# Two-layer hybrid decoder trunk: differential attention's parts share breaks in the dense matmuls, nine times a tile in place of twelve

## The reference

```
s = jnp.einsum('bhmid,bhmjd->bhmij', q_blk, k)          # m = 0, 1
s = jnp.where(dist >= 0, s - m_h * dist, -jnp.inf)
p = jax.nn.softmax(s, axis=-1)
w = p[:, :, 0] - lam_full * p[:, :, 1]
o = jnp.einsum('bhij,bhjd->bhid', w, v)
```

## Time and profile before

| | |
|---|---|
| median of 3 runs | 1976.94 us (1976.61 to 1977.6) |
| the profiled execution | 1978.86 us |
| its span, first to last instruction | 1977.0 us |
| PE busy | 1932.0 us, 98% |
| POOL busy | 920.0 us, 47% |
| DVE busy | 655.9 us, 33% |
| ACT busy | 500.0 us, 25% |
| mean granted TensorE clock | 0.995 of full speed |

### The profile page before, as it was taken

One profiled execution on the slowest core, in us unless ns is written; L12 is line 12 of the kernel. 1 busy time (PEld: TensorE's weight loads), 2 busy tenths in 40 slices (PEclk: granted clock), 3 DMA queues, 4 the chain that ended last, 5 costly groups with the idle time before them and its releaser, 6 DMA issues.

```text
span 1977.0 us, 26185 instructions
## 1 busy us (share of the span) xinstructions
PE 1932.0 (98%) x10952; PEld 1561.1 (79%) x10952; DVE 655.9 (33%) x1234; ACT 500.0 (25%) x1006; POOL 920.0 (47%) x876
## 2 busy tenths in 40 slices
PE   6999999989999999999999999999899999999999
PEld 5887777767888888777888877778688888887787
DVE  1554223122111343553335561232221113435432
ACT  3110122122222343332321011221122224433220
POOL 4555433434555444344554544434345555444454
PEclk9999999999999999999999999999999999999999
DMA  7566444535655555655675655444455555564556
GB/s 274 153 190 191 130 140 136 144 112 150 170 169 168 166 155 150 212 153 161 213 227 150 193 168 150 138 132 137 129 148 170 165 169 167 150 224 138 154 172 196
DMA packets 92181, 326.95 MB, mean 165 GB/s; under 512 B 10174, under 2 KB 10912, under 8 KB 91040
## 3 DMA queue, kind: packets, MB, share of 16 engines
q0 software_dynamic: 41472, 151.01, 27.2%
q1 hardware_dynamic: 44288, 155.75, 26.1%
q10 hardware_dynamic: 6304, 18.52, 2.4%
HBM read 316.86 MB, written 8.39 MB: 165 GB/s over the span
## 4 chain that ended last, share of the span: by engine, by line
PE 90%; DVE 5%; ACT 4%; DMA 1%; issue 0%; SPq 0%; ACTq 0%; DVEq 0%
PE acc L488 75%; PE mix L761 1%; PE mix L558 1%; DVE slots L1355 1%; PE mix L574 1%; PE mix L780 1%; PE mix L853 1%; PE mix L564 1%; PE mix L808 1%; PE mix L739 1%; DMA slots<-in_x 1%; DVE slots L1351 1%; PE mix L709 1%; PE mix L591 1%; PE mix L540 1%; ACT L1047 1%
## 5 line engine op out<-in xcount | busy, mean ns | idle before, releaser
L449 POOL TENSOR_TENSOR w_lo<-w_raw,w_hi 128x512 fp32r<-128x512 f32 x576 | 754.5, 1310 | 723.7 <-DMA w_hi<-in_wstream 509.4
L488 PE MATMUL acc<-w_hi,actT_hi 128*128 128x512 f32 x1920 | 784.5, 409 | 13.5 <-ACT slots L932 13.0
L488 PE MATMUL acc<-w_hi,actT_lo 128*128 128x512 f32 x1920 | 752.2, 392 | 0.0
L488 PE MATMUL acc<-w_lo,actT_hi 128*128 128x512 f32 x1920 | 751.2, 391 | 0.0
L488 PEld LDWEIGHTS acc<-w_hi,actT_hi 128*128 128x128 f32 x1920 | 362.1, 189 | 104.5 <-issue 33.0
L488 PEld LDWEIGHTS acc<-w_hi,actT_lo 128*128 128x128 f32 x1920 | 361.7, 188 | 78.8
L488 PEld LDWEIGHTS acc<-w_lo,actT_hi 128*128 128x128 f32 x1920 | 362.8, 189 | 65.4
L431 POOL DMA_DIRECT2D w_hi<-in_wstream x288 | 163.8, 569 | 322.5 <-PE acc L488 318.1
L488 PE MATMUL acc<-actT_hi,w_hi 128*128 128x512 f32 x384 | 152.8, 398 | 0.0
L488 PE MATMUL acc<-actT_hi,w_lo 128*128 128x512 f32 x384 | 150.3, 391 | 0.0
L488 PE MATMUL acc<-actT_lo,w_hi 128*128 128x512 f32 x384 | 150.3, 391 | 0.0
(11 more groups left out here) (249 smaller groups left out, 1646.5 us busy)
## 6 DMA issues: line engine op xcount, KB each, us to landing
w_hi<-in_wstream POOLq DMA_DIRECT2D x288, 512.0 KB, 3.9
w_raw<-in_wstream SPq DMA_DIRECT2D x288, 512.0 KB, 4.5
out_x<-slots ACTq DMA_DIRECT2D x7, 1024.0 KB, 7.6
slots<-in_x SPq DMA_DIRECT2D x4, 1024.0 KB, 15.5
slots<-in_x ACTq DMA_DIRECT2D x1, 4096.0 KB, 17.8
slots<-out_x ACTq DMA_DIRECT2D x1, 4096.0 KB, 15.4
out_x<-slots ACTq DMA_DIRECT2D x4, 256.0 KB, 2.2
cf_sb<-in_cf ACTq DMA_DIRECT2D x1, 933.0 KB, 11.0
```

What stands on the lines that cost most here:

```text
L449: pool.tensor_tensor(w_lo[:, n % RING], w_raw[:, g % RAW, k], w_hi[:, g % HI, k].bitcast(F32), ALU.subtract).then_inc(w_ready, 1)
L488: last = nc.tensor.matmul(acc[b][:, :], lhsT, rhs, start=(k == 0 and i == 0), stop=(k == kts - 1 and i == 2))
```

## The change

In each tile of differential attention the scores of head h + 2 (h = 0, 1) are issued in the break of the turn of head h, behind it, and no longer in a break of their own behind the values of head h. The turn of head 3 is issued in the break of the values of head 2, behind them. The generator has 10 stages in place of 13 (one of them, the third, issues nothing, before and after), and `project` spreads these 10 over the same k-steps. `DIF_PE`, the order of TensorE's parts, follows. The orders of ACT and DVE, all waits, and all instructions stay as they are.

```diff
-DIF_PE = ["s0", "s1", "t0", "v0", "s2", "t1", "v1", "s3", "t2", "v2", "t3", "v3"]
+DIF_PE = ["s0", "s1", "t0", "s2", "v0", "t1", "s3", "v1", "t2", "v2", "t3", "v3"]
...
                 scores(1)
                 yield
                 yield
-                for h in H:
+                for h in range(2):
                     turn(h)
+                    scores(h + 2)
                     yield
                     values(h)
                     yield
-                    if h + 2 < HEADS:
-                        scores(h + 2)
-                        yield
+                turn(2)
+                yield
+                values(2)
+                turn(3)
+                yield
+                values(3)
+                yield
...
                     project(l, 14 + n, IN_KTS + 12 * n, 12, 0, ahead=y_ready, mixer=dif(l, TILES - 1 - n),
-                            stages=13, skip=(4 if n == 0 else 0), spread=(1.0, 0.8, 0.7, 0.6)[n])
+                            stages=10, skip=(4 if n == 0 else 0), spread=(1.0, 0.8, 0.7, 0.6)[n])
```

## The result

Eight timed runs of the changed kernel gave a median of 1982.56 us (1982.15 to 1984.06), eight of the kernel before 1976.93 us (1976.23 to 1978.15): +5.6 us, a ratio of 1.0030 with a 95% interval of 1.0019 to 1.0041. Forecast were 1981.1 us and a range of 1978.5 to 1983.2.

What follows compares the result with a forecast made beforehand. TensorE, busy 98% of the span, was taken to bound the kernel. Waits adding 4.7 us less 0.6 gained by joins gave +4.1 on 1976.94, so 1981.1 us, range 1978.5 to 1983.2.

Steps and rivals of the forecast that it cites:

- 1.35 and 1.02 us: TensorE's wait for w3 before the turn of head 3, in tiles 3 and 1 of each layer; 4.7 us added.
- 0.6 us saved: Joined breaks on TensorE: 0.02 us for each of 16 turn-and-scores joins, 0.03 for each of 8 values-and-turn joins.
- The 0.09 us at the entry of the scores: Extra delay before the scores' first matmul on TensorE, claimed to stay about the same behind a turn (0.10).
- rival 3: Joining breaks saves more, the scores' entry hidden behind the turns, 2 to 2.5 us: 1979.3; chance 0.12.
- the 0.28 us to spare in tile 2: In tile 2 the turn of head 3 is reached 3.75 us behind t2, against 3.47 needed: no wait.
- POOL's phase against t2: In tiles 3 and 1, set by the k-step ending at t2, the same in both versions, so seen durations were taken.
- nothing takes it up later, since TensorE waits for no clocked event in what follows: Claim about TensorE after the new waits: the time they add is not recovered later, so the sum stays +4.1 us.
- Rival 2: The clock falls after a stall in tile 3, 6.8 us at half clock losing 3.4 us in one layer: 1984.5; chance 0.04.
- 1980.2 to 1982.0: The interval around the forecast of 1981.1 us for the whole kernel, given chance 0.66.
- rival 1: More waits: a POOL collision at L1635 in tile 2, 1 or 3, +1.5 to 2 us: 1982.8; chance 0.12.

Runs made afterwards that it cites:

- Experiment 1: From the changed kernel, only the scores of heads 2 and 3 join the turns; values of head 2 and turn of head 3 keep own breaks: 1978.2 us, ratio 1.0003.
- experiment 3: The changed kernel with all its joins, plus an empty stage between the turn of head 2 and the joined break (11 stages): 1977.55 us, ratio 1.0000.
- experiment 4: The changed kernel with ACT taking the exponentials of head 3 ahead of its copy of head 2's turns: 1978.83 us, ratio 1.0006.
- Experiment 2: From the kernel before, only the turn of head 3 joins the values of head 2; scores keep own breaks (12 stages): 1990.94 us, ratio 1.0067.
- before, second trace: The kernel before, unchanged, timed and traced a second time: 1978.16 us, ratio 1.0001.
- after, second trace: The changed kernel, unchanged, timed and traced a second time beside the kernel before: 1982.47 us, ratio 1.0029.
- experiment 7: The changed kernel plus the empty stage (no waits), with 9 extra matmuls behind the fourth output projection of each layer: 1983.03 us, ratio 1.0030.
- experiment 8: The changed kernel with 9 extra matmuls behind the fourth output projection of the first layer alone: 1983.73 us, ratio 1.0032.
- experiment 9: The changed kernel plus the empty stage (no waits), with 15 extra matmuls behind the first layer's fourth output projection alone: 1982.43 us, ratio 1.0024.

## Why the prediction was right

**The place and the cause.** t3 waits for w3 in tiles 3 and 1 and nowhere else, four times. Experiment 1 takes the waits away by giving t3 a break of its own, 3 by distance, 4 by ACT's order; all three come back to the time of before, ratios 1.0003, 1.0000 and 1.0006 (4 keeps 0.34 us of the wait in tile 3). Experiment 2 has the wait without the other join. That w3 hangs on t2 through ACT's order was argued from the earlier trace rows and is shown by 4.

**Its size.** Forecast 1.35 and 1.02 us. A joined break of values and turn costs 828.95 - 825.88 - 0.45 = 2.62 us in tile 3 of after and, counted the same way, 1.34 in experiment 3, so the wait cost 1.28; in tile 1 it is 1.62 less 0.67, 0.95. The row of waits has only 1.05 and 0.73, since it counts from the recorded end of the last matmul of the values, and t3 could have started before that end. The forecast was high by 0.07 each, in the main because t3 started 0.06 us after DVE's end and not 0.15, which the earlier trace rows gave for another wait.

**The joins.** Forecast 0.6 us saved, 0.4 measured (experiment 3). So both terms were a little off and the errors cancel: 4.46 less 0.4 is 4.1, as 4.7 less 0.6 was. The 0.09 us at the entry of the scores is kept behind a turn, as the earlier trace rows said; rival 3 is out.

**Tiles 2 and 0.** No wait, as forecast; the 0.28 us to spare in tile 2 held. The prediction put that down to POOL's phase against t2, which is kept. Experiment 2 shows what hangs on it: with t2 at another place of the k-step, POOL's subtraction met the chain in tiles 3 and 2 and added 1.09 and 1.39 us to one operation in each.

**What the sum left out.** 4.07 us in the attention stretches and 1.65 in q = 3 of the second layer make 5.72; 5.6 was timed. The claim that failed is "nothing takes it up later, since TensorE waits for no clocked event in what follows": a later wait exists, at L536, and the clock can fall behind it. The trace of before had that wait in its view of waits, with a fall behind the one of 2.1 us in the first layer and none behind the one of 1.9 us in the second; the prediction weighed only the waits of 5.6 and 1.1 us. Rival 2 had a fall of the clock, but behind the new waits. It priced it at 3.4 us, from a fall of 6.8 us, and gave it a chance of 0.04; the fall that came lasted 3.4 us and cost 1.65. Behind the new waits of about 1 us no trace shows one.

**What was luck.** The measured 1982.56 lies above the forecast's own 1980.2 to 1982.0. It is inside the range because the upper end was set past rival 1, a collision with POOL in the changed kernel that did not come; that room took in the 1.65 us of a cause that the sum did not have.

**What is shown of the second fall, and what is open.** From the start of the first layer's wait at L536 to that of the second's:

| kernel | us apart | second wait | second fall |
|---|---|---|---|
| before, second trace | 977.1 | 1.9 | no |
| experiment 3 | 977.8 | 2.2 | no |
| before | 977.9 | 1.9 | no |
| experiment 1 | 978.0 | 2.8 | no |
| experiment 4 | 978.3 | 1.9 | no |
| after, second trace | 979.3 | 2.0 | yes |
| after | 979.3 | 1.9 | yes |
| experiment 7 | 979.4 | 1.9 | yes |
| experiment 8 | 981.5 | 1.9 | no |
| experiment 2 | 985.3 | 1.9 | no |

That a fall comes at some distances and not at others, with waits of the same length, is what these traces show, one to each row (experiment 9, with its wait of 3.3 us, is left out). That the fall comes with any slower kernel is ruled out by experiments 8 and 2, slower yet and without it. Chance would hardly put all three falls between 979.3 and 979.4 us and none elsewhere, and the two kernels traced twice gave the same answer twice, but with one trace to each row it is not excluded. The first waits differ too (2.8 us in experiments 1, 3 and 4, 1.9 to 2.1 in the others), and no run varied the distance alone. Since only one run in several is traced, how often the timed runs have the fall is inferred from the medians (5.6 us in 8 runs and 5.1 in 7, both above 4.1, but with 4.1 inside both intervals). Why the distance should count was not tried.

## What to carry to other kernels

Before a wait is judged by what produces the data, follow the producer's own queue: the scores came early and it helped nothing, since ACT's copy of the turn stood ahead of their exponentials. A break in a stream of dense matmuls has nearly no price of its own here, its instructions have, so joining breaks wins next to nothing (0.4 us for 24 joins), while the half-step that it takes away between a producer and its consumer can be worth 1.3 us. And one or two microseconds added in one place can go with another clock state somewhere else: sum the stretches of the trace before putting the whole difference down to the edit.

## What the runs showed that was not expected

The clock fell behind waits of 1.9 us at L536 in one layer or in both, of the same kernel and the same length, and not behind one of 2.1 us (experiment 2, tile 3). A fall of 3.4 us cost 1.6 to 1.75 us. Beside POOL's subtraction, DVE's operation on two operands of 128x512 took 1.84 us in place of 0.75, and one on 128x1 took 1.61 in place of 0.22. From DVE's end to a matmul that waits for it passed 0.06 us here, and 0.15 in the earlier trace rows.
